# Adaptive-norm vectors in four column groups of TensorE, with a deeper ring of raw weights

## The chip, the cores and the metric

The kernel runs on one core of one Trainium2 chip. The metric is the device time of one execution in microseconds. The program is one launch; the five compute engines (TensorE, VectorE, ScalarE, GpSimd, SyncE) have instruction streams of their own and meet in semaphores.

## The reference

One inference step of a two-layer encoder, over 1024 prompt tokens and 64 sample tokens with a model width of 1024. What matters here, for each layer:

```python
mod = jax.nn.silu(c) @ w_ada + b_ada          # c: (1, 1024), w_ada: (1024, 3072)
shift, scale, gate = jnp.split(mod, 3, axis=-1)
h = rms_norm(x, g_pre) * (1.0 + scale[:, None, :]) + shift[:, None, :]
p = h @ w_in                                  # 324 + 4 * 512 + 512 + 2 * 384 columns, used in ten parts
o_a = dsa_attention(...)                      # indexer scores, top 256 keys, attention over them
o_b = retention(...)                          # 4 heads of 128
mixed = concat(o_a * silu(gate_a), head_group_norm(o_b) * silu(gate_b))
x = x + gate[:, None, :] * rms_norm(mixed @ w_out, g_post)
```

There are two vectors c, one of the prompt and one of the sample, so `silu(c) @ w_ada` is a product of 2 rows with 1024 x 3072 weights in each layer. All is float32.

## The kernel before

**Steps.** The work is cut into 180 steps: 2 layers x 10 column parts ("chunks") of the projections x 9 tiles of 128 tokens (the ninth, SAMPLE, holds the 64 sample tokens). The chunks of a layer are one for the indexer (idx), four retention heads (ret), one gate, two attention groups (att) and two halves of the output (out). All engines loop over `i` from -1 to 181 in the same order; in iteration `i` TensorE projects step `i + 1` (`project`, L844 to L847), in four quarters `q` of two k-slices each, and between the quarters does what belongs to earlier steps: `late(i - 2)` (L930, L939), `middle(i - 1, q)` (for a retention step L908 and L912, in quarter 1) and the transposes of step `i` (L823). ScalarE copies each projection out of PSUM (`take_projection`, L1072 and L1073 for retention). VectorE rotates (L1357, L1359, L1378) and does the search for the 256th largest indexer score by bisection (`count_pass`, L1438); `QUOTAS = (6.3, 5.9)` says how many of these passes each retention or gate step of layer 0 and of layer 1 takes. VectorE's L1489 takes the result of L908. In the last idx steps VectorE weighs relus of logits (L1417), which ScalarE makes (L1157) of TensorE's L860 and L861.

**Weights.** SyncE loads 128x512 slices of raw weights into a ring `w_raw` of `RAWS = 3` buffers, for the steps up to two ahead, in the order of `raw_items`: a projection slice in each of the first eight steps of a chunk, and two slices of `w_ada` in each of 32 steps (`ADA_QUOTA`). A projection slice is split by ScalarE (L1036) and GpSimd (L1246), whose semaphore `w_lo_ready` frees its buffer; a `w_ada` slice is freed by TensorE's `ada_used`. SyncE is in order: a load that waits for a buffer holds up the stores behind it.

**Adaptive-norm vectors, first part.** Shift and scale of layer 0 (`ADA_FIRST`, 32 slices: 8 k-slices of 4 groups of 512 columns) are computed at the start. SyncE streams the slices into nine buffers (L668). TensorE multiplies each with two stationary columns, silu(c) of prompt and sample, into rows 0 and 1 of four PSUM banks (L950). ScalarE copies the four results (L1186), TensorE turns them in 16 small transposes (L956), and VectorE adds the bias (L1646) and signals `mods_ready`. Nothing can be normalized before that.

**Adaptive-norm vectors, later part.** The 64 other slices (gate of layer 0, all of layer 1: `ADA_LATER`, 8 groups) are spread over 32 retention steps of layer 0, two in each, after quarters 0 and 1. Here the weight slice is stationary and silu(c) moves: four matmuls of 128x128 by 2 columns for each slice (L814), which accumulate in the bank `spare` over the whole time. At the end VectorE adds the biases in four additions (L1646) and three more operations.

Of the kernel before, what the change touches and what calls it, by code (L numbers as in the profile page):

```python
# [29 lines left out]
ALU = mybir.AluOpType  # L30
# [49 lines left out]
def step_of(l, c, t):  # L80
    return (l * NCH + c) * NT + t
# [129 lines left out]
def att_slot(i, q):  # L211
# [7 lines left out]
    if kind(j - 1) == "att":  # L219
# [20 lines left out]
ADA_END = max(g for g in range(STEPS) if len(ada_slices(g)))  # L240
# [22 lines left out]
def plan_units():  # L263

    turns, logits = ["vec"], []
    turns += [("h", 0, t, u) for t in (0, 1) for u in (0, 1)]

    for i in range(-1, STEPS + 2):
        j = i - 1
        t = lct(j)[2]  # L270
        for q in range(QUARTERS):
# [30 lines left out]
RAWS = 3  # L302
# [70 lines left out]
def build(nc, x_prompt, x_sample, cache_k_a, cache_v_a, cache_kidx_a, state_s_b, c_prompt, c_sample,  # L373
# [4 lines left out]
    with ExitStack() as ctx:  # L378
# [27 lines left out]
        cols = sb("cols", [P, 4, NHB])  # L406
# [5 lines left out]
        vec_rows = sb("vec_rows", [P, P])  # L412
        vec = sb("vec", [P, P])
        silu_c = sb("silu_c", [P, 2 * KT])
# [49 lines left out]
        ada_rows = [U[0:2, 4096 + 512 * grp:4608 + 512 * grp] for grp in range(3)] + [turned[0:2, 0, 0:512]]  # L464
# [27 lines left out]
        ada_used = sem("ada_used")  # L492
        ada_rows_ready = sem("ada_rows_ready")
# [315 lines left out]
        def _(pe):  # L809
            def ada(bank_, l, grp, k, src, a, first, col0):  # L810

                for q in range(4):
                    j = grp * 4 + q - col0
                    ins = nc.tensor.matmul(bank_[:, 2 * j:2 * j + 2], src[:, q * P:(q + 1) * P],  # L814
                                           silu_c[:, k:2 * KT:KT], start=(first and q == 0), stop=False,
                                           skip_group_check=True)
                ins.then_inc(ada_used, 1)
# [130 lines left out]
            for a, (l, grp, k) in enumerate(ADA_FIRST):  # L948
                pe.wait_ge(ada_landed[a % ADAS], 16 * (a // ADAS + 1))
                nc.tensor.matmul(ada_banks[grp][0:2, :], silu_c[:, k:2 * KT:KT], ada_raw[:, a % ADAS, :],  # L950
                                 start=(k == 0), stop=(k == KT - 1)).then_inc(ada_used, 1)
            for grp in range(4):
                pe.wait_ge(ada_rows_ready, grp + 1)
                for q in range(4):
                    j = 4 * grp + q
                    ins = nc.tensor.transpose(out_bank[:, 2 * j:2 * j + 2], ada_rows[grp][:, q * P:(q + 1) * P],  # L956
                                              ident[0:2, 0:2])
# [55 lines left out]
        def _(act):  # L1013
            nv_rows = 2 * KT + DEPTH * 40
            turns.wait_full(act, "vec")
            nc.scalar.activation(silu_c[:], turns.bank("vec")[:, 0:2 * KT], ACT.Silu)
# [174 lines left out]
            for i in range(-1, STEPS + 2):  # L1191
# [47 lines left out]
        def _(pool):  # L1239
# [32 lines left out]

            nc.gpsimd.memset(minus_half[:], -0.5).then_inc(consts_set, 1)
# [24 lines left out]
        def _(dve):  # L1298
# [348 lines left out]

            relu_count = [0]
# [20 lines left out]
            for i in range(-1, STEPS + 2):  # L1669
# [5 lines left out]
                if roots_input(i) is not None:  # L1675
                    unit = mean_squares(roots_input(i) + 1, 1, 2)
                j = i - 1
# [53 lines left out]
                if i + 1 == ADA_END:  # L1731

                    dve.wait_ge(ada_used, len(ADA_FIRST) + 1 + len(ADA_LATER))
                    fence()
                    do(modulate(0, spare, 0, 2, post_gate))
                    do(modulate(1, spare, KT, 0, pre_shift))
                    do(modulate(1, spare, 2 * KT, 1, pre_scale))
                    do(modulate(1, spare, 3 * KT, 2, post_gate))
                    fence()
                    do(nc.vector.scalar_tensor_tensor(pre_scale[:, 1], pre_scale[:, 1], 1.0, both(column(1, 1)),  # L1740
                                                      ALU.add, ALU.mult))
                    do(nc.vector.tensor_tensor(post_gate[:, 0], post_gate[:, 0], both(column(0, 2)), ALU.mult))
                    signal(nc.vector.tensor_tensor(post_gate[:, 1], post_gate[:, 1], both(column(1, 2)), ALU.mult),
                           mods_ready, 2)
# [11 lines left out]
def decay_columns():  # L1756


    out = np.zeros((P, 4, NHB))
# [33 lines left out]
```

## Time and profile before

| | |
|---|---|
| median of 3 runs | 1702.67 us (1701.23 to 1703.12) |
| the profiled execution | 1700.32 us, span 1698.5 us |
| mean granted TensorE clock | 0.966 of 2.4 GHz |
| TensorE busy | 1502.7 us, 88% |
| VectorE busy | 1208.6 us, 71% |
| ScalarE busy | 656.8 us, 39% |
| GpSimd busy | 312.7 us, 18% |
| moved by DMA | 122.12 MB, 72 GB/s in the mean |

The span goes from the first to the last instruction of the profiled execution. Busy time is the union of the records of an engine; the weight loads of TensorE (PEld) are recorded apart, since they overlap with its matmuls. An fp32 matmul leaves two records, one of the "fp32r" type leaves one. The record of a pipelined matmul is longer than the distance to the next one, so that costs are read from starts.

### The profile page before, as it was taken

How to read it: one execution, taken by the hardware profiler on the slowest of the kernel's cores; microseconds unless marked ns; L12 is line 12 of the kernel's file. 1: busy time of each engine (PE TensorE's matmuls, PEld its weight loads, DVE VectorE, ACT ScalarE, POOL GpSimd, SP SyncE). 2: the span in 40 equal slices, each digit the busy share in tenths (PEclk: the TensorE clock that was granted, in tenths of full speed). 3: DMA queues.
4: the chain of work that ended last, by engine and by line, in shares of the span. 5: the costliest groups of instructions: out<-in, count | busy, mean ns of one | idle time of the engine just before them, and what ended most of it. 6: DMA issues, size and time to landing. Idle time of an engine off the chain costs nothing.

```text
span 1698.5 us, 25555 instructions
## 1 busy us (share of the span) xinstructions
PE 1502.7 (88%) x8555; PEld 1280.2 (75%) x8555; DVE 1208.6 (71%) x3136; ACT 656.8 (39%) x1616; POOL 312.7 (18%) x277
## 2 busy tenths in 40 slices
PE   7769999999888999999966798988889699999997
PEld 1667888888667888878855776766668688988885
DVE  0787999999887656542366889999999765555224
ACT  2544222222214555554333542322222355555432
POOL 1541121222221001001134112221212100100110
PEclk9889999999998999999987999999999799999998
DMA  8202333332121112123232111111113111221224
GB/s 311 83 22 75 102 100 94 109 111 69 49 79 38 33 28 73 37 75 107 99 113 59 36 40 30 44 40 42 52 26 95 33 42 33 54 56 45 95 85 161
DMA packets 125193, 122.12 MB, mean 72 GB/s; under 512 B 33256, under 2 KB 94024, under 8 KB 125064
## 3 DMA queue, kind: packets, MB, share of 16 engines
q1 hardware_dynamic: 125064, 120.49, 23.9%
q8 instruction: 70, 1.15, 0.3%
q14 instruction: 59, 0.48, 0.1%
HBM read 93.54 MB, written 26.90 MB: 71 GB/s over the span
## 4 chain that ended last, share of the span: by engine, by line
PE 26%; DVE 25%; issue 7%; ACT 4%; DMA 4%; POOL 1%; DVEq 0%; SPq 0%; ACTq 0%
DVE U L1438 9%; PE out_bank L888 6%; PE turn L823 5%; PE proj L844 4%; PE proj L845 4%; PE proj L847 3%; DMA U<-x_dram 2%; PE logit L860 2%; PE logit L861 2%; DVE by_cos L1357 2%; DVE by_sin L1359 1%; DVE turned L1376 1%; ACT U L1165 1%; DVE q_hl L1394 1%; POOL h_lo L1252 1%
## 5 line engine op out<-in xcount | busy, mean ns | idle before, releaser
L844 PE MATMUL proj<-w_hi,h_hi 128*128 128x512 f32 (+2 forms) x1440 | 580.9, 403 | 1.9 <-POOL h_lo L1252 1.9
L845 PE MATMUL proj<-w_lo,h_hi 128*128 128x512 f32 (+2 forms) x1440 | 543.5, 378 | 0.0
L847 PE MATMUL proj<-w_hi,h_lo 128*128 128x512 f32 (+2 forms) x1280 | 482.9, 377 | 0.0
L1246 POOL TENSOR_TENSOR w_lo<-w_raw,w_hi 128x512 fp32r<-128x512 f32 (+2 forms) x160 | 202.0, 1262 | 917.1 <-ACT w_hi L1036 917.0
L1438 DVE TENSOR_SCALAR_CACHE_REDUCE U<-score,cand 128x384 bf16<-128x384 f32 x434 | 363.6, 883 | 2.4 <-DVE cand L1454 0.3
L844 PEld LDWEIGHTS proj<-w_hi,h_hi 128*128 128x128 f32 x1440 | 279.7, 194 | 33.6 <-POOL h_lo L1252 2.4
L845 PEld LDWEIGHTS proj<-w_lo,h_hi 128*128 128x128 f32 x1440 | 279.0, 194 | 32.1
L847 PEld LDWEIGHTS proj<-w_hi,h_lo 128*128 128x128 f32 x1280 | 245.3, 192 | 37.5
L823 PE MATMUL turn<-ident,U 128*128 128x128 f32 x768 | 130.0, 288 | 33.2 <-DVE U L1596 15.4
L888 PE MATMUL out_bank<-U 128*128 128x64 f32 x1248 | 156.3, 270 | 2.8 <-ACT U L1146 2.8
L1146 ACT ACTIVATE U<-turn 128x512 f32<-128x512 f32 (+3 forms) x208 | 100.7, 487 | 144.7 <-PE turn L823 100.2
L888 PEld LDWEIGHTS out_bank<-U 128*128 128x128 f32 x1248 | 151.3, 192 | 3.8 <-ACT U L1146 3.6
L1548 DVE CUSTOM_DVE_ANT_0 U<-logit,score 128x512 f32<-128x512 f32 (+3 forms) x144 | 84.6, 588 | 96.8 <-PE logit L861 85.9
L823 PEld LDWEIGHTS turn<-ident,U 128*128 128x128 f32 x768 | 97.6, 147 | 63.6 <-issue 45.0
L823 PE MATMUL turn<-ident,turned 128*128 128x128 f32 x414 | 73.0, 290 | 72.7 <-DVE turned L1376 44.2
L1165 ACT ACTIVATE U<-U,neg_max 128x128 f32<-128x128 f32 (+7 forms) x144 | 109.0, 757 | 57.0 <-DVE neg_max L1552 55.1
L860 PE MATMUL logit<-keys_hi,q_hl 128*128 128x512 f32 (+4 forms) x296 | 111.7, 377 | 20.5 <-ACT U L1157 13.6
L1110 ACT ACTIVATE U<-turn 128x256 f32<-128x256 f32 x72 | 27.7, 385 | 263.0 <-PE turn L823 263.0
L823 PEld LDWEIGHTS turn<-ident,turned 128*128 128x128 f32 x414 | 50.4, 149 | 98.1 <-DVE turned L1376 47.5
L1261 POOL TENSOR_TENSOR rstd<-means,minus_half 128x3 f32<-128x3 f32 (+2 forms) x52 | 40.2, 774 | 373.6 <-DVE means L1523 209.0
L1036 ACT ACTIVATE w_hi<-w_raw 128x512 fp32r<-128x512 f32 (+2 forms) x160 | 95.2, 595 | 34.1 <-DMA w_raw<-in_w_in_dram 18.6
L861 PE MATMUL logit<-keys_lo,q_hl 128*128 128x512 f32 (+4 forms) x296 | 104.5, 357 | 0.0
(128 smaller groups left out, 1908.5 us busy)
## 6 DMA issues: line engine op xcount, KB each, us to landing
w_raw<-in_w_in_dram SPq DMA_DIRECT2D x80, 256.0 KB, 3.0
w_raw<-in_w_ada_dram SPq DMA_DIRECT2D x64, 256.0 KB, 3.1
score<-mixed_dram SPq DMA_DIRECT2D x36, 256.0 KB, 3.0
U<-in_x_prompt_dram SPq DMA_DIRECT2D x16, 512.0 KB, 4.1
score<-in_w_ada_dram SPq DMA_DIRECT2D x32, 256.0 KB, 4.2
w_raw<-in_w_out_dram SPq DMA_DIRECT2D x32, 256.0 KB, 3.5
mixed_dram<-U SPq DMA_DIRECT2D x24, 192.0 KB, 2.1
gates_dram<-U SPq DMA_DIRECT2D x18, 256.0 KB, 2.0
```

What stands on the lines that cost most here:

```text
L823: ins = nc.tensor.transpose(turns.bank(key)[:, n * P:(n + 1) * P], piece, ident[:])
L844: nc.tensor.matmul(out, h_hi[:, k, tile], hi, start=(k == 0), stop=False)
L845: ins = nc.tensor.matmul(out, h_hi[:, k, tile], lo, start=False, stop=(t == SAMPLE and k == KT - 1))
L847: ins = nc.tensor.matmul(out, h_lo[:, k, tile], hi, start=False, stop=(k == KT - 1))
L860: nc.tensor.matmul(dst, q_hl[:, s, h, :], keys_hi[:, k0 + a:k0 + a + m], start=True, stop=False)
L861: logits.filled(nc.tensor.matmul(dst, q_hl[:, s, h, :], keys_lo[:, k0 + a:k0 + a + m], start=False, stop=True), key)
L888: ins = nc.tensor.matmul(out_bank[:, h * HD:(h + 1) * HD], probsT[:, slot, b * P:(b + 1) * P], v, start=(kb == 0), stop=(kb == nblk - 1))
L1036: nc.scalar.activation(w_hi[:, s % WS, 0:w], w_raw[:, n % RAWS, 0:w], ACT.Copy).then_inc(w_hi_ready, 1)
L1146: turns.take(nc.scalar.activation(probsT[:, u % PTS, 0:m], turns.bank(key)[:, 0:m], ACT.Copy), key)
L1165: nc.scalar.activation(probs[n % 3][:, 0:w], probs[n % 3][:, 0:w], ACT.Exp, bias=neg_max[:, n % 4:n % 4 + 1], scale=ATT_SCALE, accum_out=r ...
L1246: nc.gpsimd.tensor_tensor(w_lo[:, s % WS, 0:w], w_raw[:, n % RAWS, 0:w], w_hi[:, s % WS, 0:w].bitcast(F32), ALU.subtract).then_inc(w_lo_re ...
L1438: ins = nc.vector.tensor_scalar(found[:, n % 2, 0:valid_keys(t)], s, cand[:, j:j + 1].bitcast(F32) if b else 0.0, extra(j), ALU.is_ge, ALU ...
```

## The change

The later slices take the form of the first ones: the weight slice moves (512 columns) and silu(c) is stationary. The stationary tile `silu_c` becomes 32 columns wide for each k-slice, two of them filled and 30 zero (GpSimd zeroes it at the start, the new wait is `ada_zeroed`). Slice (grp, k) is multiplied in column group `(grp + k) % 4` of TensorE and its result goes to the 32 PSUM rows of that group; each group of rows gets two of the eight k-slices. The four groups of rows are then added up and turned in one go: ScalarE copies all 128 rows (`ada_row`, for the later part, counted by `ada_copied`), and `ada_columns` multiplies each 128x128 block of them with two columns that hold a one in rows 0, 32, 64, 96 and in rows 1, 33, 65, 97.

The later slices are now ordered group by group, four in every second retention step, 16 times, all in quarter 1 after waits for all four. A finished group is folded in the next step (`ada_group`): its fold takes a turn of the `turn` ring, and VectorE adds the bias to it at the start of the iteration (`modulate_group`), eight additions in all. The ring of raw weights grows from three to five buffers. `vec_rows`, `vec` and `silu_c` move into the scratch tile `U`.

```diff
-ADA_LATER = [(0, grp, k) for k in range(KT) for grp in (4, 5)] + \
-            [(l, grp, k) for l in range(1, DEPTH) for k in range(KT) for grp in range(6)]
-ADA_QUOTA = {step_of(0, RET0, 0) + n: 2 for n in range(NHB * NT)}
+ADA_GROUPS = [(0, 4), (0, 5)] + [(l, grp) for l in range(1, DEPTH) for grp in range(6)]
+ADA_LATER = [(l, grp, k) for l, grp in ADA_GROUPS for k in range(KT)]
+ADA_QUOTA = {step_of(0, RET0, 1) + 2 * n: 4 for n in range(NHB * NT // 2 - 1)}
...
+def ada_group(i):
+    ends = [a for a in ada_slices(i) if a % KT == KT - 1]
+    return ends[0] // KT if ends else None
...
-RAWS = 3
+RAWS = 5
...
-            def ada(bank_, l, grp, k, src, a, first, col0):
+            def ada(bank_, grp, k, src):
-                for q in range(4):
-                    j = grp * 4 + q - col0
-                    ins = nc.tensor.matmul(bank_[:, 2 * j:2 * j + 2], src[:, q * P:(q + 1) * P],
-                                           silu_c[:, k:2 * KT:KT], start=(first and q == 0), stop=False,
-                                           skip_group_check=True)
-                ins.then_inc(ada_used, 1)
+                at = 32 * ((grp + k) % 4)
+                nc.tensor.matmul(bank_[at:at + 32, :], silu_c[:, k, :], src, start=(k < 4), stop=(k >= 4),
+                                 skip_group_check=True).then_inc(ada_used, 1)
+
+            def ada_columns(out, row):
+                for q in range(4):
+                    ins = nc.tensor.matmul(out[:, 2 * q:2 * q + 2], row[:, q * P:(q + 1) * P], cols[:, 4, 0:2],
+                                           start=True, stop=True, skip_group_check=True)
+                return ins
...
-                    for a in ada_slices(i + 1)[q:q + 1]:
-                        l, grp, k = ADA_LATER[a]
-                        n = RAW_AT[("ada", a)]
-                        if a == 0:
-                            pe.wait_ge(x_squared, 2 * NT)
-                        pe.wait_ge(raw_landed[n % RAWS], raw_value(n))
-                        ada(spare, l, grp, k, w_raw[:, n % RAWS, :], a, a == 0, 16 if l == 0 else -8)
+                    if q == 1:
+                        for a in ada_slices(i + 1):
+                            n = RAW_AT[("ada", a)]
+                            pe.wait_ge(raw_landed[n % RAWS], raw_value(n))
+                        for a in ada_slices(i + 1):
+                            l, grp, k = ADA_LATER[a]
+                            if a == 0:
+                                pe.wait_ge(x_squared, 2 * NT)
+                            if k == 0 and a:
+                                pe.wait_ge(ada_copied, a // KT)
+                            ada(spare, grp, k, w_raw[:, RAW_AT[("ada", a)] % RAWS, :])
+                    if q == 0 and 0 <= i < STEPS and ada_group(i) is not None:
+                        n = ada_group(i)
+                        turns.wait_free(pe, ("ada", n))
+                        pe.wait_ge(ada_copied, n + 1)
+                        turns.filled(ada_columns(turns.bank(("ada", n))[:, 0:8], ada_row), ("ada", n))
...
-                nc.scalar.activation(ada_rows[grp], ada_banks[grp][0:2, :], ACT.Copy).then_inc(ada_rows_ready, 1)
+                nc.scalar.activation(ada_rows[grp], ada_banks[grp][:], ACT.Copy).then_inc(ada_rows_ready, 1)
...
+                if i + 1 < STEPS and ada_group(i + 1) is not None:
+                    n = ada_group(i + 1)
+                    act.wait_ge(ada_used, len(ADA_FIRST) + 1 + (n + 1) * KT)
+                    if n:
+                        turns.wait_full(act, ("ada", n - 1))
+                    nc.scalar.activation(ada_row, spare[:], ACT.Copy).then_inc(ada_copied, 1)
```

## Rows read from the trace of the kernel before

**Rows 1.** The page, part 1, busy time of each engine:
```profile
PE 1502.7 (88%) x8555; PEld 1280.2 (75%) x8555; DVE 1208.6 (71%) x3136; ACT 656.8 (39%) x1616; POOL 312.7 (18%) x277
```
**Rows 2.** Timeline of ScalarE in layer 0 (start us, us, what, idle time before):
```profile
278.77 0.28 ACT L1072 ACTIVATE U<-proj 128x128 f32<-128x128 f32 x1 [0.72 <-PE proj L847]
...
287.19 0.28 ACT L1072 ACTIVATE U<-proj 128x128 f32<-128x128 f32 x1 [0.72 <-PE proj L847]
```
**Rows 3.** Windows: 18 retention steps; length, PE, PEld, DVE, ACT, POOL; clock, DMA share, GB/s:
```profile
228.57:376.16 147.59, 147.59 (x882) 129.04 (x881) 142.35 (x413) 40.02 (x109) 31.50 (x28) 1.00 0.36 104
1057.40:1196.55 139.15, 122.21 (x594) 95.09 (x593) 134.10 (x395) 39.98 (x109) 31.63 (x28) 1.00 0.16 42
```
**Rows 4.** The same windows, L1438 alone (its records and their busy time):
```profile
228.57:376.16 147.59, 95.90 (x229) 1.00 0.36 104
1057.40:1196.55 139.15, 88.81 (x213) 1.00 0.16 42
```
**Rows 5.** VectorE's waits, 165 to 405 us (total us, times, longest us):
```profile
DVE proj L1616 <- ACT sample_low L1055: 0.6, 1, 0.6
...
DVE by_cos L1357 <- ACT rows L1073: 0.3, 1, 0.3
```
**Rows 6.** VectorE's waits in L1417, 144 to 165 us, then 982 to 1003 us:
```profile
DVE score L1417 <- ACT U L1157: 5.3, 6, 1.3
...
DVE score L1417 <- ACT U L1157: 1.3, 2, 0.9
```
**Rows 7.** Timelines of TensorE, ScalarE and VectorE, 38 to 44 us:
```profile
38.44 1.88 PE L950 MATMUL proj<-score,silu_c 128*2 128x512 f32 x4
40.16 1.88 PE L950 MATMUL logit<-score,silu_c 128*2 128x512 f32 x4
...
42.08 0.59 ACT L1186 ACTIVATE turned<-logit 2x512 f32<-2x512 f32 x1 [0.27 <-PE logit L950]
...
43.23 0.17 DVE L1646 TENSOR_TENSOR pre_shift<-out_bank,vec 128x16 f32<-128x16 f32 x1 [29.36 <-PE out_bank L956]
```
**Rows 8.** Windows of the start, columns as in rows 3:
```profile
12.00:30.00 18.00, 18.00 (x37) 3.28 (x36) 1.21 (x3) 3.98 (x10) 7.46 (x9) 1.00 1.04 380
30.00:42.50 12.50, 12.50 (x38) 2.74 (x35) 0.00 (x0) 2.18 (x4) 0.04 (x1) 1.00 0.91 295
```
**Rows 9.** The page, part 6, DMA issues (KB each, us to landing):
```profile
w_raw<-in_w_in_dram SPq DMA_DIRECT2D x80, 256.0 KB, 3.0
...
U<-in_x_prompt_dram SPq DMA_DIRECT2D x16, 512.0 KB, 4.1
```
**Rows 10.** Views of silu_c and spare (ns min/median/max, first and last start us):
```profile
L814 PEld LDWEIGHTS spare<-silu_c,w_raw x512: 187/192/192, 144.0 to 405.6; 128*128 128x128 f32 x171
...
L950 PE MATMUL proj<-score,silu_c x32: 592/592/1061, 11.6 to 39.7; 128*2 128x512 f32 x32
...
L1646 DVE TENSOR_TENSOR post_gate<-spare,vec x2: 165/170/175, 413.4 to 413.7; 128x16 f32<-128x16 f32 x2
```
**Rows 11.** Timeline of one retention step of layer 0, TensorE and VectorE:
```profile
278.57 0.40 PE L844 MATMUL proj<-w_hi,h_hi 128*128 128x512 f32 x1
...
279.73 0.39 PE L847 MATMUL proj<-w_hi,h_lo 128*128 128x512 f32 x1
...
279.96 0.95 PE L814 MATMUL spare<-silu_c,w_raw 128*128 128x2 f32 x8
...
280.76 0.47 PE L930 MATMUL out_bank<-rows,U 128*128 128x128 f32 x2
...
283.48 0.47 PE L908 MATMUL logit<-U 128*128 128x128 f32 x2
...
286.18 0.35 DVE L1489 SCALAR_TENSOR_TENSOR U<-logit,cols,causal 128x128 f32<-128x128 f32 x1
```
**Rows 12.** SyncE's waits, 100 to 450 us:
```profile
SPq L648 <- POOL w_lo L1246: 106.2, 20, 11.8
```
**Rows 13.** The view of w_raw, its last line:
```profile
DMA to landing us min/median/max: 2.0/3.0/8.0
```

More of the change, by code:

```diff
@@ L239 @@
 assert sum(ADA_QUOTA.values()) >= len(ADA_LATER)
-ADA_END = max(g for g in range(STEPS) if len(ada_slices(g)))
+def ada_group(i):
+    ends = [a for a in ada_slices(i) if a % KT == KT - 1]
+    return ends[0] // KT if ends else None
 def weight_slice(g):
@@ L270, in plan_units @@
         t = lct(j)[2]
+        if 0 <= i < STEPS and ada_group(i) is not None:
+            turns.append(("ada", ada_group(i)))
         for q in range(QUARTERS):
@@ L405, in build @@
         causal = sb("causal", [P, P])
-        cols = sb("cols", [P, 4, NHB])
+        cols = sb("cols", [P, 5, NHB])
         rows = sb("rows", [P, 4, 384])
@@ L463, in build @@
         y0 = score[:, 0:SCORE_COLS].rearrange("p (t n) -> p t n", t=NT)
-        ada_rows = [U[0:2, 4096 + 512 * grp:4608 + 512 * grp] for grp in range(3)] + [turned[0:2, 0, 0:512]]
+        ada_rows = [U[:, 4096 + 512 * grp:4608 + 512 * grp] for grp in range(3)] + [turned[:, 0, 0:512]]
+        ada_row = U[:, 5120:5632]
+        vec_rows = vec = U[:, 5632:5760]
+        silu_c = U[:, 5760:6016].rearrange("p (k n) -> p k n", n=32)
         ada_raw = score[:, 0:SCORE_COLS].rearrange("p (t n) -> p t n", t=ADAS)
@@ L492, in build @@
         ada_used = sem("ada_used")
+        ada_zeroed = sem("ada_zeroed")
+        ada_copied = sem("ada_copied")
         ada_rows_ready = sem("ada_rows_ready")
@@ L949, in _ @@
                 pe.wait_ge(ada_landed[a % ADAS], 16 * (a // ADAS + 1))
-                nc.tensor.matmul(ada_banks[grp][0:2, :], silu_c[:, k:2 * KT:KT], ada_raw[:, a % ADAS, :],
-                                 start=(k == 0), stop=(k == KT - 1)).then_inc(ada_used, 1)
+                ada(ada_banks[grp], grp, k, ada_raw[:, a % ADAS, :])
             for grp in range(4):
                 pe.wait_ge(ada_rows_ready, grp + 1)
-                for q in range(4):
-                    j = 4 * grp + q
-                    ins = nc.tensor.transpose(out_bank[:, 2 * j:2 * j + 2], ada_rows[grp][:, q * P:(q + 1) * P],
-                                              ident[0:2, 0:2])
+                ins = ada_columns(out_bank[:, 8 * grp:8 * grp + 8], ada_rows[grp])
             ins.then_inc(ada_used, 1)
@@ L1015, in _ @@
             turns.wait_full(act, "vec")
-            nc.scalar.activation(silu_c[:], turns.bank("vec")[:, 0:2 * KT], ACT.Silu)
+            act.wait_ge(ada_zeroed, 1)
+            nc.scalar.activation(silu_c[:, :, 0:2].rearrange("p k s -> p s k"),
+                                 turns.bank("vec")[:, 0:2 * KT].rearrange("p (s k) -> p s k", s=2), ACT.Silu)
             turns.take(nc.scalar.activation(vec[:, 0:nv_rows], turns.bank("vec")[:, 0:nv_rows], ACT.Copy), "vec")
@@ L1271, in gate_retained @@
                                         ALU.mult).then_inc(ret_out, 1)
+            nc.gpsimd.memset(silu_c, 0.0).then_inc(ada_zeroed, 1)
             nc.gpsimd.memset(minus_half[:], -0.5).then_inc(consts_set, 1)
@@ L1646, in modulate, with modulate_group @@
                 return nc.vector.tensor_tensor(dst[:, l], sums, both(column(l, 0)[:, what * KT:(what + 1) * KT, :]), ALU.add)
+            def modulate_group(n):
+                l, grp = ADA_GROUPS[n]
+                what, k = grp // 2, grp % 2 * 4
+                key = ("ada", n)
+                dst = (pre_shift, pre_scale, post_gate)[what][:, l, k:k + 4, :]
+                bias = column(l, 0)[:, what * KT + k:what * KT + k + 4, :].to_broadcast([P, 4, 2])
+                turns.wait_full(dve, key)
+                take(turns, nc.vector.tensor_tensor(dst, turns.bank(key)[:, 0:8].rearrange("p (k s) -> p k s", s=2),
+                                                    bias, ALU.add), key)
             relu_count = [0]
@@ L1676, in _ @@
                     unit = mean_squares(roots_input(i) + 1, 1, 2)
+                if 0 <= i < STEPS and ada_group(i) is not None:
+                    modulate_group(ada_group(i))
+                    if ada_group(i) == len(ADA_GROUPS) - 1:
+                        fence()
+                        do(nc.vector.scalar_tensor_tensor(pre_scale[:, 1], pre_scale[:, 1], 1.0, both(column(1, 1)),
+                                                          ALU.add, ALU.mult))
+                        do(nc.vector.tensor_tensor(post_gate[:, 0], post_gate[:, 0], both(column(0, 2)), ALU.mult))
+                        signal(nc.vector.tensor_tensor(post_gate[:, 1], post_gate[:, 1], both(column(1, 2)), ALU.mult),
+                               mods_ready, 2)
                 j = i - 1
@@ L1730, in _ @@
                     norm_x(0, roots_input(i), unit)
[L1731 to L1744, printed above, removed]
 def rope_tables(half):
@@ L1756, in decay_columns @@
 def decay_columns():
-    out = np.zeros((P, 4, NHB))
+    out = np.zeros((P, 5, NHB))
+    out[0::32, 4, 0] = 1.0
+    out[1::32, 4, 1] = 1.0
     i = np.arange(P)
@@ L1779 @@
     from concourse.bass_utils import run_bass_kernel_spmd
-    nc = bacc.Bacc("TRN2", target_bir_lowering=False, num_devices=1, dynamic_dma_scratch_size=1024)
+    nc = bacc.Bacc("TRN2", target_bir_lowering=False, num_devices=1, dynamic_dma_scratch_size=512)
     arrays, args = {}, []
```

3 lines of the change are left out of this document (removed).

## The prediction

> **What bounds the kernel now.** I began with the page's busy line [rows 1]: TensorE 88%, VectorE 71%. Neither share says what the stretch with the adaptive-norm work is bound by, so I went to the windows. The kernel has a natural control: layer 1 does the same retention steps without this work. The copies of projections (ScalarE) mark the steps: in layer 0 two of them lie 8.42 us apart, 278.77 and 287.19 [rows 2]; the ninth step of a head, with the sample tokens, is shorter. Two heads, 18 retention steps from such a copy to another, took 147.59 us in layer 0 and 139.15 us in layer 1 [rows 3]. In layer 0 TensorE has no idle time and in layer 1 it has 16.9 us, which looks like a TensorE bound of 8 us. VectorE says otherwise: it is busy for 142.35 and 134.10 us, so its idle time is 5.24 and 5.05 us, the same in both. The 8.4 us between the layers are VectorE work: the counting passes of L1438 alone are 95.90 us (229 records) against 88.81 us (213) [rows 4], since the quota per step is 6.3 in layer 0 and 5.9 in layer 1. The waits confirm it: from 165 to 405 us its view has three rows, of 0.6, 0.5 and 0.3 us in all, the first and the last of them in [rows 5], and none names TensorE. The two engines are matched, but VectorE is the one with nothing to give back.
>
> At the start of these steps there is a little more: from 144 to 165 us VectorE waited 5.3 us in L1417 for relus, which wait for logits, which wait in TensorE's order behind projections and the first slices; the same place in layer 1 has 1.3 us [rows 6].
>
> The start is another matter: VectorE waits 29.36 us for the first vectors and everything stands behind them. There TensorE needs 1.72 us for four records, 0.86 us a slice (38.44 to 40.16) [rows 7], and the DMA share is 1.04 until 30 us, then 0.91 to 42.5 us [rows 8]. So TensorE and the DMA engines are both the bound until about 30 us; from there TensorE alone.
>
> **The change part by part.**
>
> *First vectors, the multiplication.* A slice is still one fp32 matmul over 512 columns, now 32 instead of 2 stationary columns, in one of four column groups. No row shows two matmuls side by side. Bounds: nothing overlaps, 0.86 us a slice as now; or all four run together, 0.86 us for four. I take a value between: each of the 32 matmuls is two records, 0.43 us apart (x32 in two of the four banks, x32 in the others [rows 10]), the second must follow the first in its own group, and only then can the next group start beside it. Four slices are then 5 x 0.43 = 2.14 us alone, and 1.72 us in a stream, 0.43 us a slice. The DMA then decides. Between 12 and 42.5 us it moved 18 x 380 + 12.5 x 295 = 10.5 MB [rows 8]. The last adaptive-norm slice has about 1.6 MB behind it (two x tiles of 512 KB, two weight slices of 256 KB [rows 9]), so what it needs takes (10.5 - 1.6) / 380 = 23 us, and land near 35 to 36 us if nothing shares with it. It will share with the x tiles issued behind it, so I put the last matmul's end at 38.5 us instead of 42.0 (the bounds: 36.5 and 42.0). Gain 3.5 us.
>
> *First vectors, the fold.* Before, four ScalarE copies of 0.59 us and 16 small transposes; VectorE starts at 43.23, 1.2 us behind TensorE's end at 42.04 [rows 7]. After, the four copies come closer together than they take: 4 x 0.6 from 1.3 us before the end gives 1.2 us behind it; then the last group's four matmuls with a 128x128 load. L814 has this very shape, and takes 280.76 - 279.96 = 0.80 us [rows 11]. VectorE starts 2.3 us behind. Loss 1.1 us. Net for the start **-2.4 us** (from -4.4 to +1.1). The steps from there to 144 us hang on these vectors alone, and carry it on. The zeroing of the stationary tile on GpSimd comes before 7 us, where it is idle.
>
> *Later slices.* Before: 64 x 0.80 = 51 us of TensorE, two slices a step. After: 16 groups x 2.14 = 34 us, plus 8 folds x 0.80 = 6.4 us: TensorE gains 10.6 us, at most 31 us if four run together (13.7 + 6.4), and loses 10 us if none do (55 + 6.4). On the path of VectorE this is worth only what VectorE waits. At 144 to 165 us step 9's slices go (the first are now in step 10), and step 10 gets four instead of two: I take a third of the difference 5.3 - 1.3, **-1.4 us**. From 165 us on: **-0.5 us** of the 1.4.
>
> *Going in and out of the groups.* There are 32 places where a matmul over all 128 columns stands beside one in a group. No row has such a place. Nothing may be lost; at most TensorE stops there, and then shows the tail of a record (0.39 us long, the next 0.23 us behind it: 0.16 us [rows 11]) and an uncovered weight load of 0.19 us [rows 10]: 0.35 us each, 11 us in all, as much as the 10.6 us that it gains. I take 0.16 us, 5 us in all, which VectorE's bound hides; 0.35 is rival 5. The Trainium skill has a rule that speaks against the change here, in TensorEngine Tiling (Array Packing), Key Properties: a change of the tiling mode drains TensorE. By that rule rival 5 gains weight; the same section lets different tiles run in parallel, which speaks against rival 2. No row of the trace before shows either.
>
> *What is queued behind.* The four slices now stand at quarter 1, ahead of L908, whose result VectorE's L1489 takes: L908 starts at 283.48, 4.9 us into a step that begins at 278.57, and comes at 4.9 - 1.6 + 2.1 = 5.4 us. VectorE takes it at 286.18, 7.6 us into the step [rows 11], so this is hidden by VectorE's lag, and would cost what is over 2.2 us without it. ScalarE's new copy of 0.6 us goes into the 0.72 us for which it waits for the projection [rows 2]. VectorE's new add waits for the fold of its step, about 2.3 us into it; VectorE comes there later than that in nearly every step.
>
> *VectorE itself.* Eight adds of 0.17 us with 0.05 us of gap instead of four that start within 0.3 us and so take 0.5 us [rows 10]: 1.8 - 0.5, **+1.3 us** on the bound engine.
>
> *The ring.* SyncE waited 106.2 us for GpSimd alone to free buffers [rows 12], and no row of TensorE's waits answers to it. The fourth slice of a group takes the buffer of the weight slice of the step before, free some 3 us into that step; landing is 3.0 us in the median [rows 13], the need is 11 us into it. Slack 4 to 5 us, none if a load takes the longest 8.0 us. Cost 0.
>
> Sum: -2.4 - 1.4 - 0.5 + 1.3 = **-3.0 us**. The profiled execution is 1700.32 us (span 1698.5 and 1.8 around it), 2.4 us under the median of 1702.67; from the median the forecast is **1699.7 us**. What a measurement of this kernel can tell from no change is 0.2%, 3.4 us, so the forecast stands close to that edge.
>
> **The rivals.**
> 1. *TensorE bounds layer 0 after all.* For: no idle time, and a cadence that repeats. Against: VectorE's equal idle time [rows 3]. Then the 10.6 us go instead of the 1.9 that I take, 1702.67 - 3.0 - 8.7 = 1691. VectorE's idle time would be gone by that: 5.24 us over 18 steps are 9 us over 32. Chance 0.13.
> 2. *The column groups do not overlap.* TensorE gets 10 us more in a stretch where it has no idle time, of which VectorE's lag takes up some 2 us; with +1.1 at the start and +1.3 for the adds that is +10.4: 1713. It decides as soon as four slices take over 2 x (8.2 - 6.8) - 0.4 = 2.4 us, 8.2 being VectorE's step (147.59 / 18), 6.8 TensorE's without slices (8.42 - 1.6) and 0.4 the folds. This is the one on the other side. Chance 0.13.
> 3. *The four-at-a-time wait starves TensorE*: it stands at quarter 1 for the fourth slice, 1 us x 16: 1705 to 1715. For: the longest landing, 8.0 us. Chance 0.08.
> 4. *The start gives nothing.* The DMA engines are the bound there, the last slice ends as late as now, and the fold's 1.1 us are lost: 1702.67 + 1.1 - 0.6 = 1703, from 1701 to 1704. Chance 0.16.
> 5. *TensorE stops at each change of group*, 0.35 us 32 times. Its mean step is again 8.4 us, the 1.9 us from the waits don't come: 1701.6. For and against: nothing in the rows. Chance 0.05.
>
> My own case has 0.45, 1696 to 1702. A little over half of it is beyond the bound of 0.2%.
>
> Faster 0.25 + 0.13 = 0.38; same 0.20 + 0.16 + 0.05 = 0.41; slower 0.13 + 0.08 = 0.21. The range leaves out rival 2 and part of rivals 1 and 3, 2 in 10 in all: 1691 to 1708.
>
> **What would show it.** The first add of the vectors (L1646 before) at 40.8 us instead of 43.23; four new matmul records side by side, or 0.43 us apart; VectorE's idle time in 18 steps still near 5 us while TensorE's is no longer 0; the step of layer 0 still 8.2 us in the mean, but TensorE's steps unequal, long before a fold and short with it; no wait of TensorE for w_raw. Wrong would be: a layer 0 step under 7.9 us (rival 1), records of 0.43 us strictly in a row with steps of 8.6 us or more (rival 2), TensorE waiting for w_raw (rival 3), that add at 43 us (rival 4), a stretch without records at each change of group (rival 5).

## The result

The changed kernel took 1688.61 us in the median of 4 runs (1686.38 to 1695.29), the kernel before 1702.46 us (4 runs). The ratio is 0.9926, its 95% interval 0.9897 to 0.9955: faster, by 12.6 us (13.9 us by the medians). I had predicted 1699.7 us, and the median lies 2.4 us below my range. Two later comparisons with more runs, on two chips, found less: 0.9961 (0.9942 to 0.9980, 12 runs of the changed kernel) and 0.9956 (0.9939 to 0.9972, 10 runs), which is 6.6 and 7.5 us. Both agree with the first interval at its edge. So faster holds, and 7 us is the size that the larger samples give; the rest of the first figure stays unexplained. My forecast of 3.0 us is less than half of that too.

The page after, its busy line:

```profile
PE 1478.5 (87%) x8251; PEld 1234.9 (73%) x8251; DVE 1204.2 (71%) x3140; ACT 660.5 (39%) x1624; POOL 313.9 (19%) x278
```

TensorE has 24 us less to do than in [rows 1] and 304 instructions less. The profiled execution was the slowest of the four, 1695.29 us with a span of 1693.5 us. I use it only stage by stage, beside twelve other executions, one of them of the kernel before.

Windows of the changed kernel, the 18 retention steps of [rows 3] first, then all of layer 0's retention steps from the first to the last projection copy (columns as in rows 3):

```profile
220.76:367.42 146.66, 134.42 (x698) 99.49 (x697) 141.77 (x415) 42.37 (x114) 31.61 (x28) 1.00 0.35 105
...
151.18:435.40 284.22, 260.61 (x1350) 195.06 (x1349) 271.55 (x783) 82.41 (x222) 59.20 (x52) 1.00 0.32 95
```

And the same whole stretch in the kernel before, which I had not put among my rows:

```profile
155.25:443.63 288.38, 283.05 (x1654) 244.36 (x1654) 273.82 (x779) 78.80 (x213) 59.19 (x52) 1.00 0.32 93
```

TensorE has gone from 5 to 24 us of idle time, and the stretch from 288.4 to 284.2 us. In the 18 steps that I had chosen as the control the gain is only 0.9 us. In the nine steps before them it is 3.7 us (73.32 against 69.58), and the last eight lose 0.5. Of the 3.7 us, 2.5 come in the first two steps. Windows of these two, the kernel before and then the changed one:

```profile
155.25:171.47 16.22, 16.22 (x95) 14.16 (x95) 12.26 (x26) 5.26 (x16) 2.86 (x2) 1.00 0.33 98
```
```profile
151.18:164.93 13.75, 13.75 (x71) 10.68 (x70) 10.43 (x22) 5.21 (x16) 2.84 (x2) 1.00 0.39 116
```

Here VectorE was idle for 4.0 of 16.2 us in the kernel before, and TensorE never. TensorE has 24 records less to do in them and ends 2.5 us sooner, still without idle time.

Matmuls of the later slices in the view of `spare` (ns min/median/max, first and last start), and one batch in TensorE's timeline:

```profile
L822 PE MATMUL spare<-w_raw,U x128: 592/605/617, 153.4 to 396.2; 128*32 128x512 f32 x128
```
```profile
362.01 0.40 PE L860 MATMUL proj<-w_hi,h_lo 128*128 128x512 f32 x1
362.33 1.06 PE L822 MATMUL spare<-w_raw,U 128*32 128x512 f32 x8
363.33 0.49 PE L921 MATMUL logit<-U 128*128 128x128 f32 x2
```

Eight records of 0.6 us each fill 1.06 us together: all four column groups run at once. The next instruction starts 1.0 us behind the batch; from 362.01 the usual 0.23 us pass before it and 0.09 us more. So a batch costs 1.09 us, where four slices cost 4 x 0.80 before [rows 11].

The start, VectorE's first addition (before: 43.23, [rows 7]) and TensorE ahead of it:

```profile
41.19 0.17 DVE L1673 TENSOR_TENSOR pre_shift<-out_bank,U 128x16 f32<-128x16 f32 x1 [27.33 <-PE out_bank L828]
```
```profile
35.69 1.73 PE L822 MATMUL logit<-score,U 128*32 128x512 f32 x4
37.34 2.84 PE L828 MATMUL out_bank<-cols,U 128*128 128x2 f32 x24
40.05 1.03 PE L828 MATMUL out_bank<-cols,turned 128*128 128x2 f32 x8
```

The multiplication ends at 37.4 us instead of 42.0; the four folds then take 3.6 us in a row, the next work of TensorE starting at 40.94.

### The profile page after: what moved, and what is told of

Same layout as the page of the kernel before. It is cut to its first block, busy times and chain, and to the rows that moved or that the text cites. A ratio compares the mean times of both kernels' runs of the same rounds, so it can differ in the third digit from the quotient of the medians.

```text
span 1693.5 us, 25006 instructions
## 1 busy us (share of the span) xinstructions
PE 1478.5 (87%) x8251; PEld 1234.9 (73%) x8251; DVE 1204.2 (71%) x3140; ACT 660.5 (39%) x1624; POOL 313.9 (19%) x278
## 4 chain that ended last, share of the span: by engine, by line
PE 28%; DVE 25%; issue 6%; DMA 4%; ACT 4%; POOL 1%; DVEq 0%; SPq 0%; ACTq 0%
DVE U L1465 9%; PE out_bank L901 6%; PE turn L836 5%; PE proj L857 4%; PE proj L858 4%; PE proj L860 4%; PE logit L873 2%; DMA U<-x_dram 2%; PE logit L874 2%; DVE by_cos L1384 1%; DVE by_sin L1386 1%; DVE turned L1403 1%; DMA score<-mixed_dram 1%; POOL h_lo L1278 1%; DVE turned L1405 1%
## 5 line engine op out<-in xcount | busy, mean ns | idle before, releaser
L836 PE MATMUL turn<-ident,turned 128*128 128x128 f32 x414 | 75.3, 297 | 82.9 <-DVE turned L1403 44.9
L836 PEld LDWEIGHTS turn<-ident,U 128*128 128x128 f32 x768 | 98.5, 148 | 63.2 <-issue 44.9
```

The source lines that it names most:

```text
L836: ins = nc.tensor.transpose(turns.bank(key)[:, n * P:(n + 1) * P], piece, ident[:])
```

## The experiments

The times of this kernel spread by 10 us and more between executions, before and after: 35 runs of the kernel before on one chip lay between 1693.1 and 1709.3 us. The spread goes with TensorE's mean granted clock (correlation -0.73 in those 35, -0.6 to -0.8 in most groups of runs of one kernel). It does not touch the retention steps: kernels that do the same work there agree within 0.4 us. So each experiment is read twice: by its ratio to the kernel before on the same chip, and by the stages of its profiled execution. The stages, from starts of ScalarE's projection copies, in us. The index steps run from the first copy to the first retention copy:

```
                      first    first   index   retention, layer 0            layer 1
                      addition copy    steps   9 steps  18 steps  8    all    retention
before                43.2     54.1    101.1   73.3     147.6     67.5 288.4  267.6
after                 41.2     52.6     98.6   69.6     146.7     68.0 284.2  267.5
after, 2nd            41.7     52.5     99.7   69.6     146.7     68.0 284.3  267.5
after, 3rd            42.3     54.2    100.4   69.6     147.0     68.0 284.6  267.5
first part only       41.7     53.0     98.9   73.3     147.6     67.5 288.4  267.6
later part only       42.1     53.6     98.4   69.6     146.7     68.0 284.3  267.5
TensorE freed         42.5     54.2     96.2   68.7     145.9     68.3 282.9  267.6
one column group      41.8     53.5     96.2   77.5     154.5     67.2 299.3  267.5
rotation first, bef.  41.9     52.8     99.5   73.2     155.0     69.5 297.6  268.6
rotation first, aft.  42.1     53.3     98.3   68.3     152.4     70.4 291.1  276.5
folds early, late     42.9     53.7     98.4   69.6     146.7     68.0 284.3  267.5
folds early, early    44.9     55.7    100.0   69.6     146.8     68.0 284.3  267.5
ring of four          41.6     53.0     98.6   86.3     160.6     67.2 314.2  267.5
```

**The changed kernel again.** Unaltered.

> The changed kernel once more, unaltered, to see its spread: its profiled execution (1695.29 us) is 6 to 9 us slower than its three other runs. Theory A (the spread comes from TensorE's clock at the start, which was at its lower level longer in the profiled execution): an execution near 1687 us has its first vectors' addition before 41.2 us and the first retention copy near 145 us instead of 151.18. Theory B (the spread comes from small shifts of the order in which VectorE and the others meet later on): first retention copy at 151 us in a fast execution too, the difference arises behind 435 us. Median 1686 to 1692 by both.

Median 1693.53 us (12 runs, 1688.10 to 1700.42) against 1700.13; ratio 0.9961 (0.9942 to 0.9980). Its profiled execution was among the longer ones again (1698.42 us), so neither theory of the spread could be told by the trace of a short one. The first copy is at 152.2 us, and what is longer than in the first profile lies in layer 1's attention steps and output (443.7 us from the last retention copy to the end of the span, against 438.3). That is the place that Theory B names, but one pair of executions settles nothing.

**TensorE freed, nothing else.** The kernel before, with three of the four matmuls of each later slice left out, so that most of the later vectors are wrong.

```diff
-                for q in range(4):
+                for q in range(1):
                     j = grp * 4 + q - col0
```

> The kernel before, with one of the four 128x128 matmuls for each later slice left out of every four but the first (the vectors of the gate of layer 0 and of layer 1 are then mostly wrong): TensorE has 38 us less to do in layer 0's retention steps, all loads, waits and additions stay. This is the price of TensorE's work in that stretch alone. Theory A (VectorE is the bound there, as predicted): 1698 to 1702 us, 0.5 to 3 us under the kernel before; 18 retention steps still 146.5 to 147.6 us. Theory B (TensorE is the bound): 1688 to 1692 us, and 18 steps under 142 us.

1693.58 us, ratio 0.9961 (0.9945 to 0.9976): 6.5 us, as much as the whole change. 38 us of TensorE's work are worth 5.5 us in the retention steps (282.9 against 288.4). Both theories had their numbers wrong: the 18 steps took 145.9 us, under the 146.5 to 147.6 of Theory A and far above the 142 of Theory B. TensorE was the bound, which I had denied, but by 2% only. Behind 5.5 us something else bounds; VectorE is the busiest of the rest, with 270.8 of 282.9 us.

**First part only.** The kernel before, with the first 32 slices and their fold in the new form (`silu_c` 32 columns wide, `ada_columns`, copies of 128 rows).

> The kernel before with the first 32 slices and their fold alone in the new form; the later slices and the ring of three stay. Theory A (both parts give): about 4 us faster than before, 1698.5 us: first vectors' addition 2 us earlier, and the rest from the steps behind it. Theory B (the later part gives it all): within 1.5 us of before.

1699.32 us, ratio 0.9997 (0.9979 to 1.0015). The retention steps are to 0.1 us those of before. The first part is worth nothing that can be measured; by the interval it is at most some 4 us. Theory B held.

**Later part only.** The changed kernel, with the start as it was.

```diff
-                ada(ada_banks[grp], grp, k, ada_raw[:, a % ADAS, :])
+                nc.tensor.matmul(ada_banks[grp][0:2, :], silu_c[:, k, 0:2], ada_raw[:, a % ADAS, :],
+                                 start=(k == 0), stop=(k == KT - 1)).then_inc(ada_used, 1)
...
-                ins = ada_columns(out_bank[:, 8 * grp:8 * grp + 8], ada_rows[grp])
+                for q in range(4):
+                    j = 4 * grp + q
+                    ins = nc.tensor.transpose(out_bank[:, 2 * j:2 * j + 2], ada_rows[grp][:, q * P:(q + 1) * P],
+                                              ident[0:2, 0:2])
```

> The changed kernel with the first 32 slices in the old form (two columns, transposes): the later part and the ring of five alone. Theory A (both parts give): 1692 to 1696 us. Theory B (the later part gives it all): 1688 us, as the changed kernel. If VectorE bounds the retention steps strictly and nothing else changes: 1699 to 1702 us.

1694.57 us, ratio 0.9970 (0.9952 to 0.9987): 5.1 us, inside the 1692 to 1696 of Theory A. With the run above, the later part gives most of it or all.

**One column group.** The changed kernel with the later slices k 0 to 3 all in the first group and k 4 to 7 all in the second; the fold picks these rows.

```diff
-                at = 32 * ((grp + k) % 4)
-                nc.tensor.matmul(bank_[at:at + 32, :], silu_c[:, k, :], src, start=(k < 4), stop=(k >= 4),
+                later = bank_ is spare
+                at = 32 * (k // 4) if later else 32 * ((grp + k) % 4)
+                nc.tensor.matmul(bank_[at:at + 32, :], silu_c[:, k, :], src,
+                                 start=(k % 4 == 0) if later else (k < 4), stop=(k % 4 == 3) if later else (k >= 4),
```

> The changed kernel with the four later slices of a batch in one and the same column group (k 0 to 3 in the first, k 4 to 7 in the second); the start keeps its four groups. The result is the same, only the side-by-side run goes. One matmul takes 0.9 us, so TensorE gets 16 x 2.7 = 43 us more than the changed kernel and 14 us more than the kernel before. Theory A (TensorE bound layer 0's retention steps before, by some 4 us of 288, and the change lifted that): first to last retention copy over 295 us instead of 284.2, whole time 1703 to 1712 us. Theory B (VectorE was the bound all along, and the gain is from its own operations falling elsewhere): 284 to 289 us, whole time under 1700 us.

1707.04 us, ratio 1.0059 (1.0044 to 1.0074). A batch in TensorE's timeline:

```profile
288.68 0.39 PE L860 MATMUL proj<-w_lo,h_hi 128*128 128x512 f32 x1
289.00 3.62 PE L823 MATMUL spare<-w_raw,U 128*32 128x512 f32 x8
292.55 0.49 PE L923 MATMUL logit<-U 128*128 128x128 f32 x2
```

3.55 us instead of 1.0, so 41 us more of TensorE in 16 batches. The stretch takes 299.3 us, 15.1 more than after and 10.9 more than before. TensorE has 14 us more than before (16 x 3.64 + 8 x 0.9 = 65 against 51), and 10.9 of them come out in the time. Theory A by its numbers. This is what my rival 2 described, and its price, +10.4 us, was near (1.0059 is +10.0 us, though the start keeps its four groups here). In the changed kernel the groups do overlap, and the gain of the later part hangs on that.

**Rotation first, kernel before.** The one that looks behind VectorE's busy time.

```diff
                 if i + 1 < STEPS and weight_slice(i + 1) is not None:
+                    if kind(i) == "ret" and lct(i)[0] == 0:
+                        pool.wait_ge(rope_done, ROPE[i] + 1)
                     lower_weights(weight_slice(i + 1))
```

> The kernel before, in which GpSimd's subtraction of the weights (L1246) waits, in layer 0's retention steps, for VectorE's rotation of the same step. In the trace of before, four rotations of the first steps took 1.27 us instead of 0.43 and ended with a GpSimd record each; later ones did not. Theory A (TensorE is the bound in those steps, and VectorE's 3.4 us of longer operations only fill its slack): first to last retention copy stays at 288.4 us, VectorE's rotations are short and its idle time is larger by about 3 us. Theory B (VectorE is the bound and loses these 3.4 us to GpSimd): 285 us, and the whole time 3 us less.

1711.43 us, ratio 1.0086 (1.0068 to 1.0104), with 297.6 us in the retention steps: neither expectation. From the tenth step on the edit did something else: SyncE waits longer for GpSimd to free a buffer in a ring of three (147.6 us in L648 from 100 to 450 us, against 106.2 in [rows 12]), the slices come late, and TensorE waits for w_raw (6.5 us before weight loads and 3.6 before matmuls, neither in the kernel before). But in the first nine steps this had not yet begun, and there it answers. First the kernel before: the rotation L1378 in its groups (busy us, mean ns, idle before), and one of four such places, GpSimd and VectorE in the timeline. Then the experiment, the same group:

```profile
L1378 DVE TENSOR_TENSOR turned<-by_cos,by_sin 128x256 f32<-128x256 f32 x9 | 7.2, 805 | 1.2
```
```profile
180.21 0.43 DVE L1357 TENSOR_TENSOR by_cos<-rows,cos_b 128x256 f32<-128x256 f32 x1
180.77 1.32 POOL L1246 TENSOR_TENSOR w_lo<-w_raw,w_hi 128x512 fp32r<-128x512 f32 x1 [6.89 <-ACT w_hi L1036]
181.10 1.27 DVE L1378 TENSOR_TENSOR turned<-by_cos,by_sin 128x256 f32<-128x256 f32 x1
```
```profile
L1380 DVE TENSOR_TENSOR turned<-by_cos,by_sin 128x256 f32<-128x256 f32 x9 | 3.8, 426 | 1.2
```

The nine steps in windows, the kernel before and then the experiment:

```profile
155.25:228.57 73.32, 73.32 (x435) 63.87 (x435) 66.45 (x172) 20.91 (x58) 14.38 (x12) 1.00 0.33 97
```
```profile
152.32:225.47 73.15, 73.15 (x435) 63.94 (x435) 63.84 (x172) 20.86 (x57) 13.92 (x12) 1.00 0.30 88
```

Three things are to be seen. A rotation that meets GpSimd's record lasts 1.27 us instead of 0.43 and ends 0.28 us behind the end of that record, in all four places. Without the meeting VectorE is busy for 2.6 us less. And the time does not move, 73.32 against 73.15 us, with TensorE busy throughout. So VectorE had slack in these steps: some of it in plain sight, 6.9 us of idle time, and 2.6 us more in longer records. Theory A for the first nine steps; the other 27 are spoiled for this question.

**Rotation first, changed kernel.** The same wait in every step with a rotation.

> The changed kernel, in which GpSimd's subtraction of the weights waits for VectorE's rotation in every step that has one, in both layers. VectorE's operations are longer than the shortest of their kind by 49 us in the whole changed kernel, about 20 us of it in the rotation. Theory A (VectorE bounds the changed kernel's retention steps): up to 3 us less there, and 3 to 8 us less in all. Theory B (the waits for GpSimd only move): within 2 us of the changed kernel, or slower where a weight slice then comes late.

1701.59 us, ratio 1.0016 (1.0003 to 1.0030), and the retention steps take 291.1 and 276.5 us instead of 284.3 and 267.5. A miss for Theory A. The first nine steps gain 1.3 us, the rest lose more: VectorE is busy for 278.3 us in the stretch of layer 0 instead of 271.6. GpSimd's work had only been moved onto other records of VectorE. The rotation's mean falls from 450 to 426 ns, while this group grows from 341 ns (L1559 in the changed kernel, also x30, 8.5 us) to:

```profile
L1561 DVE TENSOR_SCALAR U<-U,mean_var,rstd 128x128 f32<-128x128 f32 x30 | 18.3, 665 | 0.0
```

So in the retention steps this order takes nothing back. Outside them this one execution was shorter than the others, 431.6 us from the last retention copy to its end against 435.8 to 443.7; whether the wait helps in the attention steps was not tested by itself.

**Folds early.** The changed kernel, with the first slices in the order of their groups, and the first three folds between the last group's slices: after its slices 5, 6 and 7, and in a second kernel, whose edit is shown, after its slices 0, 1 and 2. ScalarE's four copies wait for the end of their own group.

```diff
-ADA_FIRST = [(0, grp, k) for k in range(KT) for grp in range(4)]
+ADA_FIRST = [(0, grp, k) for grp in range(4) for k in range(KT)]
...
+                if grp == 3 and k < 3:
+                    pe.wait_ge(ada_rows_ready, k + 1)
+                    ins = ada_columns(out_bank[:, 8 * k:8 * k + 8], ada_rows[k])
```

> The changed kernel with the first 32 slices in the order of their groups, and the folds of the first three groups done between the last group's slices, so that one fold instead of four stands behind the last slice. DMA lands the slices one every 0.68 us, so there is room for the folds. If the fold is what limits the start now (TensorE ends at 37.4 and the additions begin at 41.2 us): first addition at 38.5 to 39.5 us, whole time 2 us less than the changed kernel. If x tiles and their squares limit it instead: no difference.

> As the kernel with early folds, but the three folds stand after the first three slices of the last group, not after the last three, where each slice and fold took 1 us in turn. First addition at 39.5 to 40.5 us instead of 41.2 to 42.1 if the last landing (36.3 to 37.3 us) limits it; whole time 1 to 1.5 us under the changed kernel, which is at the edge of what can be told.

0.9995 (0.9984 to 1.0006) for the first, 0.9958 (0.9941 to 0.9976) beside 0.9956 of the changed kernel for the second. No gain in either: the first addition comes at 42.9 and at 44.9 us. The first kernel's 0.9995 is above the two figures of the changed kernel. No run of the changed kernel on this chip is there to set beside it, and the stages up to the last retention step are like its own, so whether the order or the chip makes the difference stays open. In the first, slices and folds took about 1 us each in turn from 36.95 to 42.7 us, all at 2.4 GHz; so alternating costs the time that the early folds were to save. In the second something is added:

```profile
33.95 1.04 PE L822 MATMUL logit<-score,U 128*32 128x512 f32 x2
34.93 1.05 PE L828 MATMUL out_bank<-cols,U 128*128 128x2 f32 x8
35.91 1.91 PE L822 MATMUL logit<-score,U 128*32 128x512 f32 x2
37.76 1.87 PE L828 MATMUL out_bank<-cols,U 128*128 128x2 f32 x8
```

The same slice takes 1.04 us at 33.95 and 1.91 us at 35.91, the same fold 1.05 and 1.87: between them the granted clock went from 2.4 to 1.2 GHz (1.00 from 33 to 35.5 us, 0.50 from 35.9 to 42.5). That is 1.7 us of the delay; without them the addition would still not come before the changed kernel's 41.2 to 42.3 us.

**The changed kernel a third time, and a ring of four.** For the second, `RAWS = 4`.

> The changed kernel a third time, with many runs beside the kernel before. The first comparison had 4 runs of each and gave 0.9926, the second gave 0.9961 with 12. By stages, the profiled executions give -0.7 us for the first addition, about -1.6 us for the index steps of layer 0 and -4.1 us for its retention steps, 6.4 us in all. Theory A (these stages are the whole effect): ratio 0.995 to 0.997. Theory B (there is more, in stages that profiled executions showed with a spread of 3 us and more): 0.992 to 0.994.

> The changed kernel with four raw weight buffers instead of five. A batch of four then takes all the buffers, and the weight slices on either side wait for its use. Theory A (the fifth buffer keeps the loads ahead): TensorE waits for w_raw in L822, and first to last retention copy of layer 0 is 290 us or more instead of 284.3. Theory B (two steps ahead is enough): 284 to 285 us.

The first: 1693.67 us, 0.9956 (0.9939 to 0.9972), just inside Theory A's 0.995 to 0.997. The second: 1721.51 us, ratio 1.0128 (1.0094 to 1.0162), 314.2 us in the retention steps. TensorE's waits from 150 to 460 us:

```profile
PE spare L822 <- DMA w_raw<-in_w_ada_dram: 41.1, 15, 4.3
```

With four buffers a batch needs all of them, and TensorE stands 2.7 us before 15 of 16 batches. With five it has no such row. Theory A: the fifth buffer belongs to batches of four, and without it the change is a loss of some 20 us against the kernel before, 28 us behind the changed kernel on the same chip. Rival 3 was a real danger of the design, one buffer away.

## Why the prediction was wrong

**What bounds the retention steps: the step that failed.** I wrote that VectorE "is the one with nothing to give back", because its idle time was the same in 18 steps of both layers [rows 3] and its waits named no TensorE [rows 5]. From that I took 0.5 us for everything from 165 us on. Measured: 3.5 us from the second retention copy (163.78 us before, 159.08 after) to the last, and 4.1 us in the whole stretch (3.8 to 4.2 in the six executions with batches in four groups, a ring of five and no added wait). The first of these steps, up to 164 us, is part of my -1.4 us. Three things were wrong in the reading. First, TensorE's full windows and the unvarying 8.42 us [rows 2] were evidence, and I explained them away as a near tie; the one-group kernel shows that added TensorE work comes out in the time by three quarters. Second, the control of 18 steps left out the nine in which most of it happened; in the first two of them VectorE's idle time, 4.0 of 16.2 us, said plainly that it was not the bound, and for the 18 steps themselves my reading was off by 0.9 us only. Third, busy time can hold slack: in four of the nine steps VectorE's rotation was 0.84 us longer each because it met GpSimd. At 180.21 us, in one of them, VectorE began as soon as the projection copy of 0.5 us that had started at 179.69 was done, as an engine does that follows. Rival 1 (TensorE is the bound) had the right sign, but its 8.7 us were too much: the gain stops after 5.5 us, as the kernel with TensorE freed shows. That it is VectorE that stops it is argued from its busy time; no run took work from VectorE alone.

**The price of a batch.** 2.14 us forecast, 1.09 us measured, near the lower bound that I had named. TensorE gained 16 x 2.1 - 7.2 = 27 us and not 10.6. This size changed the result little: 38 us freed give only 1.4 us more in the retention steps than the change does. Rival 5 (TensorE stops at each change of group) fell: 0.09 us at the way in, not 0.35. The Trainium skill, TensorEngine Tiling (Array Packing), Key Properties, says that different tiles run in parallel, and the trace agrees, eight records in 1.06 us. It also says that changing the tiling mode drains TensorE; what the trace shows of it is this 0.09 us.

**The start.** -2.4 us forecast, about -0.6 us measured at the first addition: the mean of the seven executions with the new start and its folds at the end is 41.8 us, that of the four with the old start 42.4. The 43.23 us that I started from was the latest of those four. The multiplication gained what I forecast, 3.5 us: the turning or folding behind it starts at 41.2 us in the mean with the old start and at 37.7 with the new one. So rival 4 (the multiplication ends as late as now) fell, though its outcome, a start that gives next to nothing, came. The term that was mis-sized is the fold. I charged one of four folds behind the last slice and assumed the others in the time of the copies, a loss of 1.1 us. All four stand there, 4 x 0.9 us: from that start to the first addition it is 1.26 us in each of the four old ones and 3.8 to 5.0, in the mean 4.1, in the new ones, a loss of 2.8 us. That leaves some 0.6.

TensorE's clock differs too, but takes little here. From 42 to 54 us the granted clock is 0.86 in the profile before and 0.59 after, and over the executions 0.53 to 0.72 with the new start against 0.72 to 1.00 with the old one. Yet from the first addition to the first projection copy the mean is 11.4 us with the new start and 11.3 with the old one (10.9 and 11.4 in the first pair of profiles). No run held the clock fixed. What is left at the first projection copy is about 0.5 us, with a spread of 1.5.

**The wait at the first slices.** -1.4 us forecast for 144 to 165 us. This place lies across two stages: the index steps end at 155.25 us in the kernel before, and 3.9 us of VectorE's waits in L1417 come behind that. What the retention steps had of it is in the 4.1 us above, 0.6 us in the first of them (8.53 against 7.90 from copy to copy). Of the index steps the means over executions are 99.9 us with the old later part (three) and 98.7 with the new (nine). But the kernel with TensorE freed, which has the old order, took 96.2, and so did one with the new part; within such a spread the 1.1 us are not shown.

**The additions, and what is queued behind.** VectorE waited 0.3 us in all for a fold, and L1489's successor not at all. Their 1.3 us can't be told apart in the total: VectorE's busy time fell, by 2.3 us in the retention steps of layer 0. The ring of five cost nothing, as forecast; how near it was to costing a lot, I had put down as a chance of 0.08 and not as a matter of one buffer.

**The sum.** By stages: -0.6 at the start, -1.1 in the index steps, -4.1 in the retention steps, -5.8 us. The two larger comparisons have -6.6 and -7.5, with intervals of about 3 us to each side. The retention steps are the firm part of this; the other two are differences of means within a spread of 1.5 and 5 us. The first comparison's -12.6 us is not explained by any stage; whether it was that chip or the choice of four executions stays open. The range that I gave ended at 1691 us, 2.4 us above its median.

## What to carry to other kernels

Where two engines are both full, window the whole stretch and not a part that looks regular: here the two steps that gained most were the first, with the second engine idle for a quarter of them. An engine with slack can also hide it in records that got longer beside a third engine, so look for one operation with two durations (0.43 and 1.27 us here) before calling its engine the bound. The cheapest test of what an engine's work is worth is to leave most of it out and keep every wait: 38 us of TensorE were worth 5.5 us here in the retention steps, so a faster form of this work could give little more. When parts of a result are to be moved behind the last input, count each of them: four folds stood there, not one. When work is batched, count the buffers again: four at a time wants five.

## What the runs showed of the hardware

Four fp32 matmuls of 32 stationary columns and 512 moving ones, each in a column group of its own, took 1.0 us together, and four in one group 3.55 us, 0.89 us each. One alone between two folds took 0.98 us (33.95 to 34.93). Folding four blocks of 128 x 128 by two columns took 0.11 us a record, eight records a fold.

From 30 us on TensorE's granted clock first fell from 2.4 to 1.2 GHz between 39.5 and 43.5 us in the seven executions with the new start, between 45.5 and 48.5 us in three of the four with the old one, and not before 58.5 us in the fourth. With early folds it was at 45.0 us in one kernel and at 35.5 to 36 us in the other, in the middle of column-group matmuls alternating with folds. But the first of these kernels did the same alternation from 36.95 to 42.7 us wholly at 2.4 GHz, so what TensorE did at that moment does not tell by itself when the clock falls; its cause stays open. The spread of the whole kernel, some 15 us between its shortest and longest executions, goes with the mean granted clock: in most groups of runs 1.0 to 1.8 us for each 0.001 of it.

A VectorE addition of two operands and a GpSimd subtraction met without any semaphore between them. The addition lasted 1.27 to 1.29 us instead of 0.43 and ended 0.28 us behind the subtraction, four times out of four.
